# Feed-forward operands made with one ScalarE and one VectorE operation per chunk

## The reference

```python
y = jnp.concatenate([y_attn, u], axis=-1) @ w_o[l]
x = x + y
h2 = _rmsnorm(x, g_ffn[l])          # x * rsqrt(mean(x*x) + eps) * g
z = _dwconv(h2 @ w_up[l], w_dw_ffn[l], b_dw_ffn[l])
zg, zv = jnp.split(z, 2, axis=-1)
x = x + (jax.nn.silu(zg) * zv) @ w_down[l]
```

```python
mixed = jnp.concatenate([o_nsa, o_swa], axis=-1) @ w_out
h = h + rms_norm(mixed, attn_post_norm)
hn = rms_norm(h, ffn_pre_norm)
u = causal_dwconv(hn @ w_up, conv_w, conv_b)
gate, up = jnp.split(u, 2, axis=-1)
y = (jax.nn.gelu(gate, approximate=True) * up) @ w_down
return h + rms_norm(y, ffn_post_norm)
```

## Time and profile before

| | |
|---|---|
| median of 3 runs | 2040.1 us (2037.82 to 2045.1) |
| the profiled execution | 2033.0 us, of which the span is 2030.9 us |
| PE busy | 1914.6 us, 94% of the span |
| DVE busy | 1354.9 us, 67% |
| ACT busy | 859.3 us, 42% |
| POOL busy | 207.4 us, 10% |
| chain that ended last | PE 80%, DVE 9%, issue 6%, ACT 4% |

### The profile page before, as it was taken

One profiled execution on the slowest core, in us unless ns is written; L12 is line 12 of the kernel. 1 busy time (PEld: TensorE's weight loads), 2 busy tenths in 40 slices (PEclk: granted clock), 3 DMA queues, 4 the chain that ended last, 5 costly groups with the idle time before them and its releaser, 6 DMA issues.

```text
span 2030.9 us, 27613 instructions
## 1 busy us (share of the span) xinstructions
PE 1914.6 (94%) x9119; PEld 1515.7 (75%) x9119; DVE 1354.9 (67%) x2025; ACT 859.3 (42%) x1361; POOL 207.4 (10%) x152
## 2 busy tenths in 40 slices
PE   5989989999998998989999999898899979999998
PEld 4867768888886776768888888577556758888887
DVE  6988677777534798876777633574576267777544
ACT  4355344444323346434444422424465244444322
POOL 0300240000021200060000021000001310000010
PEclk9998999999999999999999999899799989999999
DMA  5220023333233221023333233234000213333332
GB/s 156 67 82 13 23 80 95 93 103 90 82 97 105 76 75 33 2 72 94 103 93 93 84 95 110 54 78 142 4 1 1 63 44 101 93 94 97 85 92 77
DMA packets 288986, 154.48 MB, mean 76 GB/s; under 512 B 16877, under 2 KB 287111, under 8 KB 288903
## 3 DMA queue, kind: packets, MB, share of 16 engines
q1 hardware_dynamic: 288500, 153.26, 26.3%
q10 hardware_dynamic: 403, 0.17, 0.0%
HBM read 151.31 MB, written 2.10 MB: 76 GB/s over the span
## 4 chain that ended last, share of the span: by engine, by line
PE 80%; DVE 9%; issue 6%; ACT 4%; DMA 0%; ACTq 0%; POOL 0%; DVEq 0%; POOLq 0%
PE bank L502 22%; PE bank L503 22%; PE bank L504 22%; PE bank L641 2%; PE bank L677 2%; DVE cacc L1454 2%; DVE w_lo L1332 1%; PE bank L870 1%; PE bank L891 1%; PE bank L666 1%; PE bank L914 1%; DVE tz L1343 1%; DVE h_lo L1347 1%; ACT w_hi L1036 1%; DVE pr L1716 1%
## 5 line engine op out<-in xcount | busy, mean ns | idle before, releaser
L1332 DVE TENSOR_TENSOR w_lo<-raw,w_hi 128x1024 fp32r<-128x1024 f32 (+3 forms) x345 | 400.9, 1169 | 351.5 <-ACT w_hi L1036 350.3
L1036 ACT ACTIVATE w_hi<-raw 128x1024 fp32r<-128x1024 f32 (+3 forms) x345 | 337.0, 985 | 669.5 <-PE bank L504 665.3
L502 PE MATMUL bank<-h_hi,w_hi 128*128 128x512 f32 x1448 | 580.2, 401 | 32.3 <-DVE h_lo L1347 20.3
L503 PE MATMUL bank<-h_lo,w_hi 128*128 128x512 f32 x1448 | 567.9, 392 | 0.0
L504 PE MATMUL bank<-h_hi,w_lo 128*128 128x512 f32 x1448 | 567.8, 392 | 0.0
L502 PEld LDWEIGHTS bank<-h_hi,w_hi 128*128 128x128 f32 x1448 | 273.9, 189 | 107.7 <-DVE h_lo L1347 26.5
L503 PEld LDWEIGHTS bank<-h_lo,w_hi 128*128 128x128 f32 x1448 | 274.7, 190 | 60.4 <-issue 5.5
L504 PEld LDWEIGHTS bank<-h_hi,w_lo 128*128 128x128 f32 x1448 | 274.4, 189 | 57.9
L502 PE MATMUL bank<-a_hi,w_hi 128*128 128x512 f32 x528 | 206.1, 390 | 0.0
L504 PE MATMUL bank<-a_hi,w_lo 128*128 128x512 f32 x528 | 205.5, 389 | 0.0
L503 PE MATMUL bank<-a_lo,w_hi 128*128 128x512 f32 x528 | 205.4, 389 | 0.0
(11 more groups left out here) (259 smaller groups left out, 2275.0 us busy)
## 6 DMA issues: line engine op xcount, KB each, us to landing
raw<-in_w_up SPq DMA_DIRECT2D x132, 512.0 KB, 3.8
raw<-in_w_in SPq DMA_DIRECT2D x39, 512.0 KB, 3.9
raw<-in_w_down SPq DMA_DIRECT2D x48, 384.0 KB, 3.3
raw<-in_w_down SPq DMA_DIRECT2D x48, 320.0 KB, 3.1
raw<-in_w_o SPq DMA_DIRECT2D x16, 512.0 KB, 3.4
raw<-in_cmp_w SPq DMA_DIRECT2D x8, 512.0 KB, 3.8
raw<-in_w_out SPq DMA_DIRECT2D x8, 512.0 KB, 4.9
raw<-in_w_uq SPq DMA_DIRECT2D x8, 288.0 KB, 2.9
```

The lines of the kernel that those rows point to most:

```text
L502: mm(o, wh, mh, start=start, stop=False)
L503: mm(o, wh, ml, start=False, stop=False)
L1036: last = A_(dst(w_hi), src(raw), ACT.Copy)
L1332: last = v.tensor_tensor(dst(w_lo), src(raw), dst(w_hi).bitcast(f32), ALU.subtract)
```

## The change

In both places the chunk `x * gain` is no longer written to memory. ACT reads `x` and the gain column and writes the high part at once (`gain_high`), and DVE makes the low part with one operation with three inputs, `x * gain - h_hi`. In the first place ACT also squares `x` into the four buffers of `tz` that have come free, and POOL only adds the squares of the first seven chunks to `ssq`; the eighth goes from `tz` straight into the sum matmul on PE, as `sq` did before. ACT's square of chunk `i` waits until POOL has added chunk `i - 4`, which used the same buffer. In the second place ACT also multiplies each `mix` chunk by its gain column during the projection (`mixp`, a new tile at an offset that is free by then), so that DVE's first operation there has two inputs in place of three. The matmuls are the same.

```diff
+        mixp = at("mixp", [P, KD, SEQ], 0)
...
@@ PE, first place @@
-                sums(L, Q_O, 4)
+                pe.wait_ge(ssq_done.sem, ssq_done.at(L, Q_O))
+                pe.wait_ge(rstd_done.sem, rstd_done.at(L, 4))
+                mm(STAT[:, :], ones[:, :], ssq[:, :], start=True, stop=False)
+                pe.wait_ge(xs_done.sem, xs_done.at(L, KD))
+                mm(STAT[:, :], ones[:, :], tz[:, (KD - 1) % 4, :], start=False, stop=True).then_inc(stat_done.sem, 1)
@@ ACT @@
+            def gain_high(L, n_x, m, gain):
+                act.wait_ge(x_done.sem, x_done.at(L, n_x))
+                A_(h_hi[:, m, :], x[:, m, :], ACT.Copy, scale=gain).then_inc(op_hi.sem, 1)
...
                 for i, m in enumerate(O_ORDER):
                     if i % 2 == 1:
                         split(L, g, S_O + 4 + i // 2 + SPL)
-                    op_high(L, KD + KQ + KKV + i, h_hi[:, m, :], i)
+                    gain_high(L, i + 1, m, lc[:, C_GFFN + m:C_GFFN + m + 1])
+                    if i == 0:
+                        act.wait_ge(u_lo.sem, u_lo.at(L, KC))
+                    if i >= 4:
+                        act.wait_ge(ssq_done.sem, ssq_done.at(L, Q_O - KD + i - 2))
+                    A_(tz[:, i % 4, :], x[:, m, :], ACT.Square).then_inc(xs_done.sem, 1)
...
                     A_(xsq[:, c % 4, :], x[:, c, :], ACT.Square).then_inc(xsq_done.sem, 1)
-                    if high is not None:
-                        op_high(N, high + c, h_hi[:, c, :], 2 + c % 2)
+                    if gains is not None:
+                        gain_high(N, nx + c + 1, c, cols[:, gains + c:gains + c + 1])
...
                 A_(mix[:, m, :], bank[m % 2][:, :], ACT.Copy).then_inc(mix_done.sem, 1)
+                act.wait_ge(mix_done.sem, m + 1)
+                A_(mixp[:, m, :], mix[:, m, :], ACT.Copy, scale=cols[:, C2_APOST + m:C2_APOST + m + 1]).then_inc(mixp_done.sem, 1)
@@ DVE, first place @@
-                    v.tensor_tensor(h_lo[:, O_ORDER[i], :], tz[:, i % 4, :], h_hi[:, O_ORDER[i], :].bitcast(f32), ALU.subtract)\
-                        .then_inc(op_lo.sem, 1)
+                    m = O_ORDER[i]
+                    v.scalar_tensor_tensor(h_lo[:, m, :], x[:, m, :], col(C_GFFN + m), h_hi[:, m, :].bitcast(f32),
+                                           ALU.mult, ALU.subtract).then_inc(op_lo.sem, 1)
...
                     if i >= 1:
                         low(i - 1)
-                    dve.wait_ge(x_done.sem, x_done.at(L, i + 1))
-                    v.tensor_scalar(tz[:, i % 4, :], x[:, m, :], col(C_GFFN + m), None, ALU.mult).then_inc(op_f.sem, 1)
@@ DVE, second place @@
             dve.wait_ge(rstd_done.sem, rstd_done.at(N, 5))
-            for i in range(KD + 3):
+            dve.wait_ge(mixp_done.sem, KD)
+            for i in range(KD + 2):
...
-                    v.scalar_tensor_tensor(tz[:, i % 2, :], mix[:, i, :], cols[:, C2_APOST + i:C2_APOST + i + 1], rstd[:, 0, :],
-                                           ALU.mult, ALU.mult).then_inc(op2.sem, 1)
+                    v.tensor_tensor(tz[:, i % 2, :], mixp[:, i, :], rstd[:, 0, :], ALU.mult).then_inc(op2.sem, 1)
...
-                if i >= 3:
-                    c = i - 3
+                if i >= 2:
+                    c = i - 2
                     dve.wait_ge(op_hi.sem, op_hi.at(N, 2 * KD + c + 1))
-                    v.tensor_tensor(h_lo[:, c, :], tz[:, 2 + c % 2, :], h_hi[:, c, :].bitcast(f32), ALU.subtract).then_inc(op_lo.sem, 1)
-                if 2 <= i <= KD + 1:
-                    c = i - 2
-                    dve.wait_ge(x_done.sem, x_done.at(N, KD + c + 1))
-                    if c >= 2:
-                        dve.wait_ge(op_lo.sem, op_lo.at(N, 2 * KD + c - 1))
-                    v.tensor_scalar(tz[:, 2 + c % 2, :], x[:, c, :], cols[:, C2_FPRE + c:C2_FPRE + c + 1], None,
-                                    ALU.mult).then_inc(op_f.sem, 1)
+                    v.scalar_tensor_tensor(h_lo[:, c, :], x[:, c, :], cols[:, C2_FPRE + c:C2_FPRE + c + 1], h_hi[:, c, :].bitcast(f32),
+                                           ALU.mult, ALU.subtract).then_inc(op_lo.sem, 1)
@@ POOL, first place @@
-                squares(L, Q_O - KD, KD, lambda c: x[:, O_ORDER[c], :],
-                        lambda c: pool.wait_ge(x_done.sem, x_done.at(L, c + 1)), 5)
+                zero(L, 5)
+                for c in range(KD - 1):
+                    pool.wait_ge(xs_done.sem, xs_done.at(L, c + 1))
+                    pool.wait_ge(ssq_done.sem, ssq_done.at(L, Q_O - KD + c + 1))
+                    p.tensor_tensor(ssq[:, :], ssq[:, :], tz[:, c % 4, :], ALU.add).then_inc(ssq_done.sem, 1)
```

More of the change, by code:

```diff
@@ L41 @@
 Q_VAR = Q_CKV + KC + 1
-Q_O = Q_VAR + KD + 1
+Q_O = Q_VAR + KD
 Q_DN = Q_O + KD + 1
@@ L283, in build @@
         rstd_done = tally("rstd_done", 0, 5)
+        xs_done = tally("xs_done", 0, KD)
         lc_done = tally("lc_done", 0, 1)
-        op_f = tally("op_f", 0, 2 * KD + KQ + KKV)
+        op_f = tally("op_f", 0, KD + KQ + KKV)
         op_hi = tally("op_hi", 0, 2 * KD + KQ + KKV)
@@ L343, in build @@
         op2 = tally("op2")
-        mix_done = tally("mix_done")
+        mix_done, mixp_done = tally("mix_done"), tally("mixp_done")
         act_link, dve_link, pool_link = sem("act_link"), sem("dve_link"), sem("pool_link")
@@ L1203, in _, with squares_ring @@
             N = DEPTH
-            def squares_ring(nx, use, high=None):
+            def squares_ring(nx, use, gains=None):
                 for c in range(KD):
@@ L1296, in _ @@
                 A_(mix[:, m, :], bank[m % 2][:, :], ACT.Copy).then_inc(mix_done.sem, 1)
+                act.wait_ge(mix_done.sem, m + 1)
+                A_(mixp[:, m, :], mix[:, m, :], ACT.Copy, scale=cols[:, C2_APOST + m:C2_APOST + m + 1]).then_inc(mixp_done.sem, 1)
             inv_root(N, 5, 0, D)
-            squares_ring(KD, 1, 2 * KD)
+            squares_ring(KD, 1, C2_FPRE)
             inv_root(N, 6, 0, D)
@@ L1807, in _ @@
             pool.wait_ge(fixed.sem, 1)
-            with link.loop(DEPTH, KQ + KKV + KC + 2 * KD - 5) as L:
+            with link.loop(DEPTH, KQ + KKV + KC + KD - 4) as L:
                 squares(L, Q_CQ - KQ, KQ, lambda c: craw[:, c, :], lambda c: pool.wait_ge(c_copy.sem, c_copy.at(L, c + 1)), 1)
```

## The result

| | kernel before | changed kernel |
|---|---|---|
| median of the runs compared | 2037.82 us (2029.15 to 2045.1, 7 runs) | 2023.74 us (2020.93 to 2030.1, 7 runs) |
| ratio | | 0.9941, 95% interval 0.9919 to 0.9963 |
| profiled execution, its span | 2033.0 us, 2030.9 us | 2023.64 us, 2021.5 us |

Faster by 14.1 us between the medians, where 13.1 us were forecast. The ratio is that of the means (2036.9 and 2025.0 us), 12.0 us or 0.59%. The median shown ahead of the prediction was that of three of the seven runs of before.

A forecast was written before the change was run, and what follows sets the result against it. The prediction took DVE, slowed beside POOL, to bound the first place, with PE waiting. Gains of 12.1 us (first place, two layers) and 1.0 us (second) sum to 13.1, from 2040.1 to 2027.0 us; range 2021 to 2034.

The forecast's parts named there:

- First place, 6.0 us per layer: Projection's second half: PE stops waiting for DVE and reaches the sum matmul 6.0 us sooner per layer, 12.1 for two.
- Its prices: First place, durations assumed per operation: high part 0.71 us, square 0.62, POOL's add 1.30, low part 0.67, split 1.15.
- The last `h_lo`: End of the first place: done at 283.1, while PE wants it at 284.7, a margin of 1.6 us.
- the multiply's 0.49 us at 261.84: First place: DVE's multiply read as 0.49 us when running alone, against 1.26 us beside POOL.
- rival 1: First place: the shared port stays the bound, each layer wins only 2.6 us, median 2033.9; chance 7%.
- rival 2: First place: POOL's adds become the bound and close the buffer ring, so the kernel is slower, 2047; chance 3%.
- rival 3: First place: PE then waits for a load or ACT, so only the second place counts, 2039; chance 2%.
- `mixp` costs nothing: Ahead of the second place: ACT's extra 0.71 us copy is done before POOL's square, the sum and the root.
- the 0.13 forecast for the earlier start: Second place, behind the root: two-input operations bring the first add, first square and PE's start 0.13 us forward.
- Second place, 1.0 us: Second place: PE's 0.86 us wait for the first `h_lo` goes and it starts 0.13 us earlier, together 1.0 us.
- PE is then held by its own sum matmul, 1638.07 + 2.04: Second place: with the low part sooner, PE's own sum matmul at half clock holds it until 1640.1 less 0.13.
- its upper bound (3): Second place: the gain could be 3 us if the earlier start shortens the 7 us at granted clock 0.53.

The follow-up runs named there:

- joining alone: Kernel before with only DVE's multiply removed in the first place (three-input low part, high part from x on ACT), POOL still squaring and adding: 2033.09 us, ratio 0.9976.
- the fills: Changed kernel plus a POOL fill of zeros, which only writes, behind each of the first six adds of the first place: 2023.73 us, one run.
- the added reads: Changed kernel plus one POOL multiply per chunk in the first place, whose result nothing reads: 2025.07 us, one run.
- the first place alone: Changed kernel with the second place as in the kernel before: 2023.83 us, ratio 0.9937.
- squares alone: Kernel before with only ACT squaring into its own four buffers and POOL only adding in the first place; DVE keeps its multiply: 2028.26 us, ratio 0.9942.
- the second place alone: Kernel before with only the second place changed (`mixp` and the joined operations): 2035.93 us, ratio 0.9983.

## Why the prediction was right, and which term was not

- **First place, 6.0 us per layer: right.** 6.06 measured in both layers. Alone, the first place makes the whole difference that the totals can show.
- **Its prices.** High part 0.71 us (mean 0.716 over 16), square 0.62 (0.616), POOL's add 1.30 (1.296, 14 of them, so seven a layer), low part 0.67 free and up to 1.4 beside POOL (0.74 in the record, mean 0.79), split 1.15 (1.22). The last `h_lo` was forecast to be over 25.1 us after the stretch's first matmul (283.1 - 258.03); it was over at 280.08, 25.2 after. One reading was loose: the multiply's 0.49 us at 261.84 wasn't taken alone, since a POOL square began at 261.96. The price holds, 0.48 at 1638.57 with POOL idle.
- **The port, rival 1, failed by timing, not by mechanism.** A POOL instruction that reads and a DVE operation with two SBUF inputs do exclude each other, the new low part with them (1.81 us at most with joining alone). But seven adds of 1.30 us fall mostly into DVE's waits for PE and its adds from a bank. The rule of the Trainium skill that the prediction weighed ("SBUF — State Buffer", "Who interferes with whom") also says that a GpSimd instruction that only writes doesn't contend; the fills show that (1.22 and 0.74 us beside them), and the added reads show its other half (2.06 us).
- **POOL's ring, rival 2, and a wait for loads or ACT, rival 3:** no sign of either. Every add took about 1.30 us, and PE's stretch has no bracket at all.
- **`mixp` costs nothing: right.** From POOL's first square of `mix` to the second place's start the changed kernel needs no longer (42.44 before, 42.32 after), and the 0.12 us less are the 0.13 forecast for the earlier start.
- **Second place, 1.0 us: mis-sized, it was 2.1.** The first `h_lo` came when forecast: 3.96 us after the first multiply started (1627.93 to 1631.89), 1.7 sooner than before's 5.67, for a forecast of 1.8. The step that failed is "PE is then held by its own sum matmul, 1638.07 + 2.04": the price of the wait was read from the bracket, 0.86 us. The bracket begins at the modelled end of a matmul, and the next matmul doesn't wait for that end: it started 0.75 us ahead of it, as soon as `h_lo` was there. By starts the operand matmul came 1.30 us after the sum matmul instead of 2.90, so 1.6 us. The remaining 0.4 between the sum matmuls came from the clock. Before, PE was granted half of full speed until about 1644.6, 6.6 us from its start (windows: 0.50 up to 1644.0, then 0.68 in one us, then 1.00; the earlier trace rows has 0.53 over nearly the same stretch). After, it was half until about 1634.3, 3.7 us from the start, and the second chunk took 2.26 us instead of 2.70. The prediction had that in its upper bound (3) but took the term without it.
- **The total and the profile.** The median came out 3.3 us under the forecast 2027.0: 1.0 us is the change, and 2.3 us are that the median of before fell from 2040.1 to 2037.82 with four more runs. The profiled span was forecast as 2017.8 us and was 2021.5, because of the differences in unchanged code above. That the medians hit so well is in part luck: by the means the kernel won 12.0 us, by its places 14.2.

As the span of a run goes with its granted clock, one slope was laid through the 91 runs on record that have a clock, all kernels with a level of their own: 1.45 us less for each 0.001 of clock, 1.4 us of scatter left. At equal clock the changed kernel is 12.0 us below before, the first place alone 11.5, joining alone 7.6, squares alone 8.7 (each within about 1.2), and the second place alone 0.7 above (within 1.0). The order and the rough sizes are those of the traces, but each is 0.6 to 3 us less than its places give. The clock is in part an outcome of the waits that were removed, and so the division is no proof. **Open:** whether the 2 us of the second place arrive in the total. The traces show them in five kernels; no total does. Open too is why the clock of the unchanged attention differs from execution to execution.

## What to carry to other kernels

Lay the helper engine's work for one turn against the bound engine's time for the same turn, and stop there: two edits that each bring it near that time don't add. In this chip's records a slow DVE operation with two SBUF inputs is explained by what POOL was reading at that moment, and moving that read away is worth as much as removing a DVE operation. Price a wait of PE from start to start, not from the bracket, and look when the tile that it needs landed; and before reading a difference of two profiles, subtract it piece by piece at landmarks, since unchanged code moved by 6 us here.

## What was not expected of the hardware

- A matmul wait shown as 0.86 us in brackets was worth 1.6 us by starts, behind a 128x512 sum matmul at half clock.
- The longer gap right behind PE's first matmul of the second place went together with a longer slow phase. With 2.90 us from that matmul to the next, PE stayed at half of full speed for 6.0 to 7.2 us from its start (four profiles); with 1.30 us, for 2.9 to 3.9 us (five profiles). The times are estimates from windows of about one us. Nothing here shows what decides it.
- The last piece of the second block's attention, about 300 matmuls, took from 47.6 to 53.7 us in nine profiles, with a granted clock of 0.93 and 0.76 in the two that are compared.
